# A decoder layer with grouped experts: bf16 slot tables made before the rows are turned, and three smaller changes of order

## The reference

```python
h = rmsnorm(x, norm1_g) * (1 + scale1) + shift1          # scale, shift, gate from silu(c) @ w_ada
q_a, k_a, v_a, q_b, k_b, v_b, q_i, k_i, w_i, g_a, g_b = split(h @ w_in)
o_a = stick_breaking_attention(q_a, k_a, v_a)            # 8 heads of 64
score = sum_h w_i[h] * relu(q_i[h] @ k_i.T)              # indexer, causal
sel   = top_k(score, 128)                                # keys per query
o_b   = softmax attention of q_b over the selected k_b, v_b, with a bias by distance
x = x + gate1 * ((sigmoid(g_a) * (o_a @ w_o_a) + sigmoid(g_b) * (o_b @ w_o_b)) @ w_out)
h2 = rmsnorm(x, norm2_g) * (1 + scale2) + shift2
probs = softmax(h2 @ router_w + router_b)                # 16 experts in 4 groups
# best group by the sum of its two largest, then two experts in it, weights w_e
x = x + gate2 * sum_e w_e * ((silu(h2 @ w_gate[e]) * (h2 @ w_up[e])) @ w_down[e])
```

## Time and profile before

| | |
|---|---|
| median of 3 runs | 822.87 us (821.62 to 823.71) |
| the profiled execution | 822.21 us |
| its span, first to last instruction | 820.5 us |
| TensorE busy | 758.8 us, 92% |
| DVE busy | 613.8 us, 75% |
| ACT busy | 430.8 us, 53% |
| DMA | 184.93 MB, mean 225 GB/s |

### The profile page before, as it was taken

One profiled execution on the slowest core, in us unless ns is written; L12 is line 12 of the kernel. 1 busy time (PEld: TensorE's weight loads), 2 busy tenths in 40 slices (PEclk: granted clock), 3 DMA queues, 4 the chain that ended last, 5 costly groups with the idle time before them and its releaser, 6 DMA issues.

```text
span 820.5 us, 9963 instructions
## 1 busy us (share of the span) xinstructions
PE 758.8 (92%) x3614; PEld 580.1 (71%) x3616; DVE 613.8 (75%) x802; ACT 430.8 (53%) x519; POOL 115.9 (14%) x90
## 2 busy tenths in 40 slices
PE   3899999999999879999999988999999999999982
PEld 3777777776655546667888866787878787888862
DVE  4676886633999995552666566989989999999980
ACT  6335225256575445556333243766767776676660
POOL 4020000000010000001000011216123241313111
PEclk9799999999999999999999999999999999999997
DMA  9928997110130221125329137999999999999933
GB/s 286 332 63 312 380 370 272 52 52 1 52 103 1 66 88 52 52 61 190 112 101 358 79 129 277 412 386 403 369 387 387 388 387 388 388 371 379 384 92 56
DMA packets 87307, 184.93 MB, mean 225 GB/s; under 512 B 8112, under 2 KB 27672, under 8 KB 85216
## 3 DMA queue, kind: packets, MB, share of 16 engines
q1 hardware_dynamic: 79200, 156.29, 51.0%
q0 software_dynamic: 8064, 28.09, 11.9%
HBM read 171.74 MB, written 12.62 MB: 225 GB/s over the span
## 4 chain that ended last, share of the span: by engine, by line
PE 47%; DVE 26%; DMA 12%; issue 6%; ACT 6%; SPq 1%; POOL 1%; DVEq 1%; ACTq 0%; POOLq 0%
PE ps L662 12%; PE ps L664 11%; PE ps L663 11%; DVE w_lo L1928 7%; DMA gx<-rows_scratch,slot_tok 7%; DMA out<-ys,slot_tok 3%; DVE score L1749 3%; DVE m L1748 2%; ACT w_hi L1484 2%; DVE w_lo L1579 2%; DMA raw<-in_w_in 2%; DVE ys L2028 2%; PE ps L916 1%; ACT w_hi L1223 1%; DVE score L1735 1%
## 5 line engine op out<-in xcount | busy, mean ns | idle before, releaser
L1928 DVE TENSOR_TENSOR w_lo<-raw,w_hi 128x2048 fp32r<-128x2048 f32 x80 | 179.4, 2283 | 4.3 <-ACT w_hi L1484 4.2
L1484 ACT ACTIVATE w_hi<-raw 128x2048 fp32r<-128x2048 f32 x80 | 150.8, 1914 | 3.6 <-PE ps L664 3.6
L662 PE MATMUL ps<-w_lo,hgT_hi 128*128 128x512 f32 x256 | 102.4, 400 | 2.8 <-DVE hgT_lo L2050 1.0
L662 PE MATMUL ps<-act_lo,w_hi 128*128 128x512 f32 x232 | 98.6, 425 | 5.5 <-issue 2.8
L663 PE MATMUL ps<-w_hi,hgT_lo 128*128 128x512 f32 x256 | 99.9, 390 | 0.0
L664 PE MATMUL ps<-w_hi,hgT_hi 128*128 128x512 f32 x256 | 99.8, 390 | 0.0
L664 PE MATMUL ps<-act_hi,w_hi 128*128 128x512 f32 x232 | 91.5, 394 | 0.0
L663 PE MATMUL ps<-act_hi,w_lo 128*128 128x512 f32 x232 | 91.3, 394 | 0.0
L1223 ACT ACTIVATE w_hi<-raw 128x2048 fp32r<-128x2048 f32 (+2 forms) x29 | 51.9, 1793 | 69.1 <-DMA raw<-in_w_in 46.0
L1579 DVE TENSOR_TENSOR w_lo<-raw,w_hi 128x2048 fp32r<-128x2048 f32 (+2 forms) x29 | 61.9, 2144 | 31.4 <-ACT w_hi L1223 31.2
L616 POOL DMA_INDIRECT out<-ys,slot_tok x15 | 50.3, 3356 | 134.0 <-DVE ys L2028 132.2
(11 more groups left out here) (278 smaller groups left out, 1387.0 us busy)
## 6 DMA issues: line engine op xcount, KB each, us to landing
raw<-in_w_down SPq DMA_DIRECT2D x32, 1024.0 KB, 15.3
raw<-in_w_gate SPq DMA_DIRECT2D x30, 1024.0 KB, 18.2
raw<-in_w_up SPq DMA_DIRECT2D x18, 1024.0 KB, 19.8
raw<-in_w_in SPq DMA_DIRECT2D x16, 1024.0 KB, 6.3
raw<-in_w_ada SPq DMA_DIRECT2D x16, 1024.0 KB, 7.2
raw_late<-in_w_up SPq DMA_DIRECT2D x14, 1024.0 KB, 16.3
raw<-in_w_ada SPq DMA_DIRECT2D x8, 512.0 KB, 6.8
raw_early<-in_w_ada SPq DMA_DIRECT2D x8, 512.0 KB, 5.3
```

The lines of the kernel that those rows point to most:

```text
L662: pe.matmul(o, a[0], b[1], start=start, stop=False)
L1484: act.activation(e_hi[s_][:, :], e_raw[r][:, :], ACT.Copy).then_inc(e_top, 1)
L1928: dve.tensor_tensor(e_lo[s_][:, :], e_raw[r][:, :], e_hi[s_][:, :].bitcast(F32), ALU.subtract).then_inc(e_split, 1)
```

## The change

Five parts. (1) `slot_t` and `sel` become bfloat16. The token's number is stored less 256, and 256 is added on reading; the weight is stored in three bf16 parts in columns 1 to 3 and no longer in two, so DVE has two more instructions there, and the clearing of the table goes. (2) `slot_table` goes ahead of `turn_rows` and `down` on TensorE, and `slot_index` ahead of `hg_low` on DVE. (3) The 8 rounds that are left over are done in units 5 to 8 and not in units 1 to 4. (4) At the last expert DVE's order becomes: silu product, split of chunk nz, first half of hidT_lo, split of chunk nz + 1, `scaled` of the expert before, second half of hidT_lo (it was: split nz, silu product, split nz + 1, the two halves, `scaled`); `down_last` waits for its second chunk only when it comes to it. (5) `keep_clock` has three calls ahead of the first table and four behind it, in place of one and three.

```diff
--- before.py
+++ after.py
@@ -159,7 +159,7 @@
     ys = at("ys", [D], F32, 160)
     ys_last = at("ys_last", [D], F32, 164)
     gx = [at(f"gx{i}", [D], F32, 164 + 4 * i) for i in range(2)]
-    sel = [at(f"sel{i}", [NT, P], F32R, (200, 172)[i]) for i in range(2)]
+    sel = [at(f"sel{i}", [NT, P], BF16, (200, 172)[i]) for i in range(2)]
     silu = at("silu", [F_EXP], F32, 178)
     hidT_hi = at("hidT_hi", [4, P], F32R, 180)
     hidT_lo = at("hidT_lo", [4, P], F32R, 198)
@@ -180,7 +180,7 @@
 
     ident = tiny("ident", [P])
     ones = tiny("ones", [P])
-    slot_t = at("slot_t", [NT, N_EXP, 4], F32R, small[0])
+    slot_t = at("slot_t", [NT, N_EXP, 4], BF16, small[0])
     negones = tiny("negones", [P])
     negtri = tiny("negtri", [P])
     posm = at("posm", [NT, N_EXP], F32, small[0])
@@ -1131,12 +1131,13 @@
 
                 pe.wait_ge(hidT_sp, X + 1)
                 pe.wait_ge(y_sb, 2 * X)
-                pe.wait_ge(e_split, z + 2)
+                pe.wait_ge(e_split, z + 1)
                 for n in range(2):
                     for f in range(4):
                         s_ = (z0 + f // 2) % E_SPL
                         a = D * (f % 2) + 512 * n
                         if n == 0 and f == 2:
+                            pe.wait_ge(e_split, z + 2)
                             pe.wait_ge(hidT_sp2, turn)
                         m = three(ps[5 + n][:, :], (hidT_hi[:, f, :], hidT_lo[:, f, :]),
                                   (e_hi[s_][:, a:a + 512], e_lo[s_][:, a:a + 512]), f == 0, f == 3)
@@ -1171,19 +1172,19 @@
                     turn_hid(X)
                     down(X - 1, z0 + 4, z + 4, (1,))
                     return
+                if b == 0 and more_:
+                    slot_table(X + 2, e + 2)
                 turn_rows(X + 1, 1 - b)
                 if not first_:
                     down(X - 1, z0 + 4, z + 4)
                 turn_hid(X)
-                if b == 0 and more_:
-                    slot_table(X + 2, e + 2)
 
             def expert_pass(X0, turn):
                 if isinstance(X0, int):
-                    keep_clock(1, ps[6][:, :].rearrange("p (c s) -> p c s", c=4), 4)
+                    keep_clock(3, ps[6][:, :].rearrange("p (c s) -> p c s", c=4), 4)
                 slot_table(X0, 0, True)
                 if isinstance(X0, int):
-                    keep_clock(3, ps[6][:, :].rearrange("p (c s) -> p c s", c=4), 4)
+                    keep_clock(4, ps[6][:, :].rearrange("p (c s) -> p c s", c=4), 4)
                 turn_rows(X0, 0)
                 stage(X0, 0, 0, True, False)
                 stage(X0 + 1, 1, 1, False, False)
@@ -1825,7 +1826,7 @@
                     rows(p + 1)
                 normal(p)
                 gate_splits(FILL_A[-1] if p == 0 else FILL_B[p - 1])
-                topk_rounds(2)
+                topk_rounds(0 if p < 4 else 2)
                 if p >= 3 and p % 2:
                     ob_low((p - 3) // 2)
             assert not rounds
@@ -1877,8 +1878,7 @@
                 link(dve.scalar_tensor_tensor(out=amp2c[:, :], in0=sc2c[:, :], scalar=1.0, in1=g2c[:, :], op0=ALU.add,
                                               op1=ALU.mult))
                 dve.tensor_tensor(rwm[:, :, :], rw[:, :, :], amp2c[:, :].unsqueeze(2).broadcast_to([P, KD, N_EXP]), ALU.mult)
-                link(dve.memset(slot_t[:, :, :, :].bitcast(F32), 0.0))
-                dve.tensor_copy(slot_t[:, :, :, 0], tid[:, :].unsqueeze(2).broadcast_to([P, NT, N_EXP]))
+                dve.tensor_scalar(slot_t[:, :, :, 0], tid[:, :].unsqueeze(2).broadcast_to([P, NT, N_EXP]), -float(S // 2), None, ALU.add)
                 dve.tensor_copy(shb[:, :, :], sh2c[:, :].unsqueeze(2).broadcast_to([P, KD, P])).then_inc(prep_ok, 1)
 
             def amp_row():
@@ -1990,7 +1990,9 @@
             wts = r_pr[:, :, :].rearrange("p (t g) e -> p t (g e)", t=NT)
             link(dve.tensor_tensor(wts, wts, r_tot[:, :].unsqueeze(2).broadcast_to([P, NT, N_EXP]), ALU.mult))
             link(dve.tensor_copy(slot_t[:, :, :, 1], wts))
-            dve.tensor_tensor(slot_t[:, :, :, 2], wts, slot_t[:, :, :, 1].bitcast(F32), ALU.subtract).then_inc(tab_ok, 1)
+            link(dve.tensor_tensor(wts, wts, slot_t[:, :, :, 1], ALU.subtract))
+            link(dve.tensor_copy(slot_t[:, :, :, 2], wts))
+            dve.tensor_tensor(slot_t[:, :, :, 3], wts, slot_t[:, :, :, 2], ALU.subtract).then_inc(tab_ok, 1)
 
             dve.wait_ge(pos_ps, 1)
             dve.tensor_copy(counts[:, :], ps[5][:, NT * N_EXP:(NT + 1) * N_EXP])
@@ -2021,8 +2023,8 @@
                 dve.wait_ge(ws_ps, X + b + 1)
                 if again:
                     dve.wait_ge(scat, 16 * (X - N_EXP + 1 + b))
-                dve.tensor_copy(slot_tok[:, bass.ds(e + b, 1)], ps[7][:, 4 * b:4 * b + 1])
-                dve.tensor_reduce(slot_w[:, bass.ds(e + b, 1)], ps[7][:, 4 * b + 1:4 * b + 3], AX.X, ALU.add).then_inc(idx_ok, 1)
+                dve.tensor_scalar(slot_tok[:, bass.ds(e + b, 1)], ps[7][:, 4 * b:4 * b + 1], float(S // 2), None, ALU.add)
+                dve.tensor_reduce(slot_w[:, bass.ds(e + b, 1)], ps[7][:, 4 * b + 1:4 * b + 4], AX.X, ALU.add).then_inc(idx_ok, 1)
 
             def scaled_part(dst, e, n):
                 dve.scalar_tensor_tensor(out=dst[:, 512 * n:512 * n + 512], in0=ps[5 + n][:, :],
@@ -2062,29 +2064,33 @@
                 if not first_:
                     low_e(z + 4, z0 + 4)
                     low_e(z + 5, z0 + 5)
-                low_e(nz, nz0)
+                if last_ is None:
+                    low_e(nz, nz0)
                 dve.wait_ge(silu_ok, X + 1)
                 dve.wait_ge(e_used, z + 4)
                 if not isinstance(X, int) or X >= 1:
                     dve.wait_ge(hidT_ps, X)
                 dve.tensor_tensor(silu[:, :], ps[1][:, :], silu[:, :], ALU.mult).then_inc(hid_ok, 1)
+                if b == 0 and more_:
+                    for j in range(2):
+                        slot_index(X + 2, e + 2, again, j)
                 if last_ is None:
                     hg_low(X + 1, 1 - b)
-                low_e(nz + 1, nz0 + 1)
                 if last_ is not None:
+                    low_e(nz, nz0)
                     dve.wait_ge(hidT_h, X + 1)
                     dve.tensor_tensor(hidT_lo[:, 0:2, :], ps[4][:, 0:2 * P].rearrange("p (k s) -> p k s", k=2),
                                       hidT_hi[:, 0:2, :].bitcast(F32), ALU.subtract).then_inc(hidT_sp, 1)
+                    low_e(nz + 1, nz0 + 1)
+                    scaled(X - 1, e - 1, 0)
                     dve.wait_ge(hidT_h2, last_)
                     dve.tensor_tensor(hidT_lo[:, 2:4, :], ps[4][:, 2 * P:4 * P].rearrange("p (k s) -> p k s", k=2),
                                       hidT_hi[:, 2:4, :].bitcast(F32), ALU.subtract).then_inc(hidT_sp2, 1)
                     return
+                low_e(nz + 1, nz0 + 1)
                 dve.wait_ge(hidT_h, X + 1)
                 dve.tensor_tensor(hidT_lo[:, :, :], ps[4][:, :].rearrange("p (k s) -> p k s", k=4),
                                   hidT_hi[:, :, :].bitcast(F32), ALU.subtract).then_inc(hidT_sp, 1)
-                if b == 0 and more_:
-                    for j in range(2):
-                        slot_index(X + 2, e + 2, again, j)
                 low_e(nz + 2, nz0 + 2)
 
             def expert_pass(X0, turn):
@@ -2110,7 +2116,6 @@
                     stage(X0 + q * 2 + 1, q * 2 + 1, 1, False, False, None, again)
                 stage(X0 + N_EXP - 2, N_EXP - 2, 0, False, False, None, again, False)
                 stage(X0 + N_EXP - 1, N_EXP - 1, 1, False, False, turn, again)
-                scaled(X0 + N_EXP - 2, N_EXP - 2, 0)
                 scaled_last(X0 + N_EXP - 1, N_EXP - 1, turn)
 
             expert_pass(0, 1)
```

## The result

The changed kernel takes 817.23 us (median of 4 runs, 815.99 to 818.03) beside 823.09 for the kernel before (821.62 to 823.71): a ratio of 0.9936, 95% interval 0.9918 to 0.9953. That is 5.9 us faster by the medians and 5.3 by the ratio. Three single runs (one each of the kernel before, of order_only and of after_again) took 50 to 700 us longer than the others of their kernel and are left out of medians and ratios. The forecast was 814.0, its range 812 to 818. The profiled execution took 817.70 us with a span of 816.0, which is 4.5 us less than the 820.5 of before. The prediction had 8.9 for the same difference.

What follows compares the result with a forecast made beforehand. In the loop DVE, DMA and the pair time lay within a few per cent, so waits decide. Selection -0.3, head +0.5, loop -8.2, capped to 7.1 together; last expert -1.8: 8.9 off 822.87 gives 814.0 us, range 812.0 to 818.0.

Steps and rivals of the forecast that it cites:

- The gather in the loop: Expert loop: gather issued 4 us earlier, TensorE's waits for gx (6.0 us) go, 0.3 given back, gain 5.7 us.
- The bf16 tables in the loop: Expert loop: table products start 0.07 us apart for 0.11, saving 0.36 per pair, 2.5 us (0 to 4.5).
- The cap: Expert loop: weight stream gets no faster, so compute comes forward only 7.15 us before DVE stalls on landings.
- The sign that I had named: Expert loop: pair periods near 36.4 us, the last ones near 38, would show the forecast right.
- Rival 2: Loop: cap bites earlier, as in-order ACT waiting for a landing holds silu and hgT_hi; 816.3 us, chance 0.2.
- Rival 3: Loop: DVE becomes the bound, a pair shrinks by 0.6 us only; 817.1 us, chance 0.14.
- Rival 4: Loop: the full queue makes the earlier gather land no earlier; 821 us at worst, chance 0.06.
- rival 5: Loop: earlier gathers among the weight loads lengthen the stream; slower, 829 us at 2 us per pair, chance 0.05.
- The head: Start of the expert part: compute +0.5 us; first gather issued, and weight stream shifted, 0.35 later.
- The selection rounds: Attention units: first four end 4.6 us sooner, stall at the seventh; gain 0.3 us (gain 1.1 to loss 0.6).
- The last expert: Last expert: silu turned at 792.9 for 794.43, last down product 1.8 us earlier; gain 1.8 us (1.0 to 2.2).
- rival 1: Loop: as forecast, the weight stream caps the gain; 814.0 us, itself 812.5 to 815.5, chance 0.55.

Runs made afterwards that it cites:

- order_only: The kernel before with slot_table ahead of turn_rows and slot_index behind the silu product, tables still fp32: 818.9 us, ratio 0.9963.
- after_again: The changed kernel measured once more, beside the same runs of the kernel before: 816.6 us, ratio 0.9941.
- bf16_only: The kernel before with the slot tables in bf16 and the DVE operations that go with them, order unchanged: 826.04 us, ratio 1.0048.
- fill_clock: The changed kernel with seven calls of unread products behind the first table in place of four: 816.52 us, ratio 0.9933.
- split_later: The changed kernel with the first DVE split of the expert part behind hgT_lo and not ahead of it: 814.48 us, ratio 0.9904.
- sel_back: The changed kernel with the selection rounds as in the kernel before: 816.15 us, ratio 0.9924.
- fill_light: The changed kernel with seven unread-product calls behind the first table and w_down loads halved from the fifth expert on: 816.53 us, ratio 0.9938.
- combo_tail: Changed kernel, selection rounds as before, first split behind hgT_lo, three and five unread-product calls, two more ahead of the last down product: 813.55 us, ratio 0.9899.

## Why the prediction held, and where it was wrong

**The gather in the loop: right.** The move of 4 us came (the issue is at 666.24, its pair's rows are needed at 678.79), the waits went, and order_only shows the move worth 3 us of time. The stall that they uncover, 0.41 us in every pair, I had as 0.3 once, in the first stage alone: 2.6 us too little given back. The gather is also shorter than the 9.2 us that I expected, 6.8, since it now goes out under hgT_lo, which reads the matmul buffer, and not under a split. That changed nothing in the time, as with 9.2 us it would have landed at 675.4, still 3.4 ahead of its use.

**The bf16 tables in the loop: right in kind, half in size.** 0.68 us per pair, not 0.36: the four-column products start 0.025 apart, below the 0.03 that I had as the lower bound, and the 0.07 of a 128-column product that I priced them by does not bound them. That is 4.8 us in seven pairs for 2.5, 2.3 more than I had, and it covers the stall's 2.6: the loop's sum came out right because two wrong terms nearly cancelled, which is luck. Alone they give 1.0 us (bf16_only); after the order is changed they are on the path and bring the rest of the loop's 7.7. The parts are not a sum: 1.0 and 4.0 alone (order_only's loop, 259.7 to 255.7), 7.7 together.

**The cap: the mechanism is there, but did not bind in this kernel.** I forecast that compute would meet the landings after 7.15 us. The head was late, so compute came only 1.8 us forward at the last rows, and the stream itself moved back: the copy of the last pair's first w_gate chunk starts at 769.00 in both, but after it starts on the landing, 764.2 before; 4.8 us later, 4.1 of them from the first gather's later landing, which the loads wait for. 0.6 us of DVE's lead were left. The sign that I had named, last pairs near 38 us, did not come: the last one takes 36.4. With anything more ahead of it, the cap bites at once: fill_clock loses 1.1 us of 1.6, split_later 0.9 of 3.0, and a stream lighter by a sixth takes the 1.1 away. Rival 2 (ACT in order holds silu behind a landing) is refuted at that place: in the changed kernel ACT starts five copies on landings and TensorE waits for none of it. Rival 3 (DVE the bound) is half true: 0.4 us per pair are DVE's, but the pair shrank by 0.8 us and not by its 0.6. Rival 4 is out, as the gather lands 5.7 us ahead of its use, and so is rival 5, with steady pairs of 36.6 us.
By the Trainium skill ("DMA: Bandwidth & Descriptors", Bandwidth) the ports would allow 435 GB/s. The loop's steady pairs in the windows here and in the earlier trace rows had 384 and 385, and fill_clock's last landings were late at 384; the measurement decides. Only where the loop begins do two slices of the page show more, 413 GB/s.

**The head: the step that failed.** I wrote that the first gather is issued 0.35 later and let it keep its 4.2 us. It was issued later by about that (0.38 in bf16_only, 0.36 from the ninth unit in after_again; 0.70 in the first profile), but I had priced the shorter products of the first table alone, 0.16 us. Those of the second let DVE's split of 2.28 us begin 0.30 us before POOL's instruction and not 0.12 after it. In all eight profiles with the bf16 tables and the split at that place the instruction takes 2.88 or 2.89 us; in the three with fp32 tables and the three with the split moved it takes 1.03. split_later and bf16_only are the proof from both sides. It costs 1.8 us, and it moves the stream with it. The kernel before had shown the same hold in its loop, where the first gather of a pair began 0.2 us behind a split:

```profile
632.15 2.93 POOL L624 DMA_INDIRECT gx<-rows_scratch,slot_tok  x1 [11.37 <-DVE slot_w L2025]
```

The Trainium skill ("SBUF — State Buffer", Who interferes with whom) says that a DVE operation with both inputs in SBUF contends with a GpSimd instruction that reads SBUF, and that whichever starts first holds the other off. The trace agrees with it for POOL, 1.03 us or 2.88 by which begins first. It does not for DVE: every split that begins under a gather's or scatter's instruction takes 2.27 to 2.29 us, as the others do. The same section infers that a tensor_tensor leaves descriptor generation alone; for this gather, which reads its rows' numbers from SBUF, the 2.88 us say otherwise.
The other 1.6 us of the head are the half clock. I had set it on the unread products, as in the earlier trace rows; it came 0.05 us behind the first product of the experts (505.34), after 3 us without one. fill_clock and after_again, where no half clock lies on the first expert's products, take 13.30 and 13.34 us there for 14.89, which shows that it is this.

**The selection rounds: the mechanism right, the bounds too narrow.** The wait went from unit 3 to unit 7 and the first four units ended 4.5 us sooner, all as forecast. For a second stretch at half clock I had a loss of 0.6; it was 1.35, and two stretches came. With one stretch, as in after_again, the ninth unit stands where it stood before: 41.60 for 41.58. So the forecast gain of 0.3 is not there: the move is worth nothing, plus or minus one stretch of about 1.6 us. The rule of the Trainium skill ("TensorE: Matmul & The Clock Gate", The HAM clock gate) that activity lifts the throttled state fits the stretches, all of which follow idle time; that idle time brings one each time does not follow, as sel_back shows.

**The last expert: right.** Silu is turned 1.6 us sooner behind the last rows and the last down product starts 1.8 sooner (26.40 us for 28.22), in the changed kernel and alone. The rest of the 2.69 is the last scatter, 6.5 us for 7.3. It is not the edit's: bf16_only, which leaves the last expert as it was, has 6.4, so the kernel before's one profile had a long one. What the time shows of the edit is 0.8 to 1.2 us, since a half clock may follow the wait that stays.

The time hit the range because the loop and the last expert gave 10.4 us for a forecast of 9.1, while all ahead of the loop took 5.9 for 0.2. So part of the hit is luck. The measured 817.2 lies outside the 812.5 to 815.5 of my own rival 1 and at the 817.1 of rival 3, but the 5.9 us that brought it there are in neither; the range reached so far only because I had widened it for rivals 2 and 3.

## What to carry to other kernels

Look at what else runs when a GpSimd gather or scatter is issued: a DVE operation with both inputs in SBUF that began just before it held it off until it ended (2.88 us for 1.03 here), and an edit that let DVE reach that operation 0.4 us sooner brought this about. When parts of a change are tested alone, a part that loses alone (the tables, +4 us) can be right in the whole, and its loss may be repaired at its own place, here by moving one line (split_later). Where compute runs close behind a stream of loads, ask of each gain whether the stream moves with it.

## What was not expected of the hardware

- The hold of POOL is not a delay of the transfer: from the end of POOL's instruction to the landing it is 3.1 us in both kernels (495.90 to 499.05, 500.07 to 503.18). In all profiles every gather's instruction that began under a split ended 0.8 to 0.9 us after the split's end, and one that began under hgT_lo took 0.9 to 1.0.
- From the attention units on, TensorE's granted clock fell from 2.4 to 1.2 GHz for 3.4 or 6.8 us at a time, mostly after idle stretches of 1.9 to 3.2 us (those near 484 and 495 us also after pairs of gaps of 0.6 to 1.3), but not after each: sel_back had the same 2.8 us wait as the kernel before and kept its clock. After the 2.1 to 2.3 us ahead of the last down product it fell on that product in 6 of 13 profiles. Each stretch of 3.4 us on products costs about 1.6 us. I take that for most of what the runs of one kernel scatter by (2 us for the changed one), but the runs without a profile don't show it. What decides it is open. With the idle time filled by unread products it stayed away from the products behind them in fill_clock, fill_light and combo_tail, but so few runs can't tell that from chance: in after_again it stayed away from the first expert without them.
- Matmuls of four bf16 columns start 0.025 us apart, those of four fp32r columns 0.11.
